# Output projections of two attention-like blocks as three products of split operands in place of one fp32 product

## The reference

```python
for l in range(DEPTH):                      # 2
    z = rmsnorm(x, g_mix[l]) @ w_in[l]      # 1024 -> 3080
    c_b, c_c, c_v, q, k, v, f_logit = jnp.split(z, SPLITS, axis=-1)
    y_conv = rmsnorm per 64 channels of short_gated_conv(c_b, c_c, c_v, conv_w[l])   # 512 channels
    y_fox = rmsnorm per head of forgetting_attention(q, k, v, log_f)                 # 8 heads x 64
    x = x + jnp.concatenate([y_conv, y_fox], axis=-1) @ w_out[l]                     # 1024 -> 1024
    hx, m = rmsnorm(x, g_xa[l]), rmsnorm(mem, g_mem[l])
    x = x + mem_cross_attention(hx, m, ...) @ w_xo[l]                                # 4 heads x 128 -> 1024
    hf = rmsnorm(x, g_ffn[l])
    x = x + (swiglu(hf, ...) if l == 0 else moe_swiglu(hf, ...))                     # 2816 wide; 8 experts, top 2
```

## Time and profile before

| | |
|---|---|
| median of 3 runs | 1675.71 us (1674.78 to 1680.75) |
| profiled execution, span | 1677.9 us |
| PE, DVE, ACT busy | 93%, 60%, 50% |
| front of layer 0, layer 1 (to the first channel mixer product) | about 0 to 305 us, 510 to 823 us |
| mean granted PE clock | 0.928 |

### The profile page before, as it was taken

One profiled execution on the slowest core, in us unless ns is written; L12 is line 12 of the kernel. 1 busy time (PEld: TensorE's weight loads), 2 busy tenths in 40 slices (PEclk: granted clock), 3 DMA queues, 4 the chain that ended last, 5 costly groups with the idle time before them and its releaser, 6 DMA issues.

```text
span 1677.9 us, 19256 instructions
## 1 busy us (share of the span) xinstructions
PE 1553.3 (93%) x7547; PEld 1257.9 (75%) x7547; DVE 1013.2 (60%) x820; ACT 844.6 (50%) x730; POOL 58.0 (3%) x59
## 2 busy tenths in 40 slices
PE   6999987899997999977799999999999999999998
PEld 5987654778877977655778777787777877778776
DVE  3334233444344334333578788787787877878777
ACT  4423222443433313222476766766677666676674
POOL 3020000000001020000000000000000000000000
PEclk8987789899997978788699999999999999999999
DMA  8321041445542412031298988989889798897987
GB/s 279 126 76 51 25 169 35 175 152 201 197 151 75 139 64 76 29 141 69 103 357 296 340 334 305 361 291 341 343 301 354 297 345 334 309 352 293 340 345 287
DMA packets 86444, 371.48 MB, mean 221 GB/s; under 512 B 7444, under 2 KB 36224, under 8 KB 69504
## 3 DMA queue, kind: packets, MB, share of 16 engines
q1 hardware_dynamic: 86400, 370.84, 60.1%
HBM read 369.78 MB, written 1.05 MB: 221 GB/s over the span
## 4 chain that ended last, share of the span: by engine, by line
PE 80%; DVE 7%; ACT 6%; issue 5%; SPq 1%; DVEq 0%; POOL 0%; DMA 0%; POOLq 0%; ACTq 0%
PE bank L1232 41%; PE bank L1228 18%; PE bank L1229 18%; ACT wh L617 3%; DVE wl L861 2%; ACT ffn L813 1%; PE bank L1240 1%; DVE ffn L1176 1%; DVE xres L1197 1%; ACT aT L646 1%; DVE xn L844 1%; DVE scratch L978 0%; ACT L614 0%; ACT xn L607 0%; PE bank L1394 0%
## 5 line engine op out<-in xcount | busy, mean ns | idle before, releaser
L861 DVE TENSOR_TENSOR wl<-ring,wh 128x2816 fp32r<-128x2816 f32 (+2 forms) x245 | 751.4, 3076 | 294.7 <-ACT wh L617 279.4
L617 ACT ACTIVATE wh<-ring 128x2816 fp32r<-128x2816 f32 (+2 forms) x245 | 623.0, 2549 | 446.3 <-PE bank L1229 355.0
L1228 PE MATMUL bank<-wh,xh 128*128 128x512 f32 (+1 forms) x960 | 364.7, 380 | 17.9 <-issue 7.3
L1229 PE MATMUL bank<-wh,xl 128*128 128x512 f32 (+1 forms) x960 | 355.9, 377 | 0.0
L1228 PEld LDWEIGHTS bank<-wh,xh 128*128 128x128 f32 x960 | 181.9, 189 | 71.5 <-DVE xres L1197 11.2
L1232 PE MATMUL bank<-wl,xh 128*128 128x512 f32 (+1 forms) x960 | 227.9, 375 | 0.0
L1229 PEld LDWEIGHTS bank<-wh,xl 128*128 128x128 f32 x960 | 182.0, 190 | 32.1
L1232 PEld LDWEIGHTS bank<-wl,xh 128*128 128x128 f32 x960 | 171.1, 189 | 27.6
L1228 PE MATMUL bank<-wh,ah 128*128 128x512 f32 x440 | 173.0, 393 | 0.8 <-DVE al L878 0.8
L1229 PE MATMUL bank<-wh,al 128*128 128x512 f32 x440 | 171.3, 389 | 0.0
L1232 PE MATMUL bank<-aT,wh 128*128 128x256 f32 x448 | 116.8, 296 | 2.1 <-DVE aT_low L879 2.1
(11 more groups left out here) (212 smaller groups left out, 1338.7 us busy)
## 6 DMA issues: line engine op xcount, KB each, us to landing
ring<-in_we_gate SPq DMA_DIRECT2D x68, 1408.0 KB, 7.2
ring<-in_we_up SPq DMA_DIRECT2D x64, 1408.0 KB, 7.9
ring<-in_we_down SPq DMA_DIRECT2D x56, 1536.0 KB, 7.9
ring<-in_w_in SPq DMA_DIRECT2D x16, 1536.0 KB, 7.7
ring<-in_w_gate SPq DMA_DIRECT2D x8, 1408.0 KB, 6.1
ring<-in_w_up SPq DMA_DIRECT2D x8, 1408.0 KB, 5.9
ring<-in_w_down SPq DMA_DIRECT2D x6, 1536.0 KB, 6.4
ring<-in_w_xkv SPq DMA_DIRECT2D x8, 1024.0 KB, 5.2
```

What stands on the lines that cost most here:

```text
L617: nc.scalar.activation(wh[:, j, 0:n], ring[:, slot, 0:n], ACT.Copy).then_inc(high_ready, 1)
L861: nc.vector.tensor_tensor(wl[:, j, 0:n], ring[:, slot, 0:n], wh[:, j, 0:n].bitcast(F32), ALU.subtract).then_inc(low_ready, 1)
L1228: nc.tensor.matmul(dst, x_high, w_high, start=first, stop=False)
L1229: return nc.tensor.matmul(dst, x_low, w_high, start=False, stop=False)
```

## The change

All fills, those of `wo` and `xo` too, are now split, so that the two buffers of `wh` and `wl` are also used for them, and their ring slots are free when the low half is made. The operand `yT` is gone. For the convolution's half DVE scales in place in `zc`, ACT copies to `aT`, and DVE subtracts into `aT_low`. For the attention's half ACT scales from the bank into `aT`, DVE subtracts into `aT_low`. For the memory attention's output ACT copies from the bank to `aT`, DVE subtracts into `aT_low`. `token_projection` makes, for each slot of two k tiles, 16 products with the high half of the weights (activation high and low) and then 8 with the low half.

```diff
     used_count, slots_used_total = {}, 0
-    split_names = [n for n in fill_names if n[1] not in ("wo", "xo")]
+    split_names = fill_names
     split_at = {n: i for i, n in enumerate(split_names)}
...
         mem_gained = xn[:].rearrange("p t (k s) -> p (t k) s", s=S)
-        yT = xn[:].rearrange("p t (k s) -> p (t k) s", s=S)
         xsc = part(5120, XH, 2, S)
...
         acthigh_ready = sem("acthigh_ready")
+        yconv_ready = sem("yconv_ready")
+        yhigh_ready = sem("yhigh_ready")
+        ylow_ready = sem("ylow_ready")
         stored = sem("stored")
...
                     nc.scalar.activation(pT[:, h, :], bank(l, f"pt{h}")[:, 0:3 * P], ACT.Copy).then_inc(take(l, f"pt{h}"), 1)
+                high_of(l, "wo", 0, 1)
+                for i in range(2):
+                    act.wait_ge(*full(l, f"mv{i}"))
+                act.wait_ge(yconv_ready, l + 1)
+                for i in range(2):
+                    nc.scalar.activation(aT[:, 2 * i:2 * i + 2, :], zc[:, 2 * i:2 * i + 2, :], ACT.Copy).then_inc(yhigh_ready, 1)
                 for i in range(2):
...
+                high_of(l, "wo", 2, 3)
+                for i in range(2):
+                    act.wait_ge(*full(l, f"oT{i}"))
+                    for k in range(2):
+                        c = 4 + 2 * i + k
+                        ins = nc.scalar.activation(aT[:, c, :], bank(l, f"oT{i}")[:, k * S:k * S + S], ACT.Copy,
+                                                   scale=col(l, "fox", 2 * i + k))
+                    ins.then_inc(yhigh_ready, 1)
                 high_of(l, "xq", 0, 1)
...
                 square(l, "xq", sq[:, 0:4, :], zqk[:, 0:4, :])
+                high_of(l, "xo", 0, 1)
                 guess_rows(l, "xq", "ssxq", mxq[:])
...
                     act.wait_ge(*full(l, f"xo{i}"))
-                    nc.scalar.activation(zqk[:, 4 + 2 * i:6 + 2 * i, :].rearrange("p a s -> p (a s)"),
-                                         bank(l, f"xo{i}")[:], ACT.Copy).then_inc(take(l, f"xo{i}"), 1)
+                    nc.scalar.activation(aT[:, 2 * i:2 * i + 2, :].rearrange("p a s -> p (a s)"),
+                                         bank(l, f"xo{i}")[:], ACT.Copy).then_inc(yhigh_ready, 1)
...
                     for j in (2 * i, 2 * i + 1):
-                        ins = nc.vector.scalar_tensor_tensor(yT[:, j, :], zc[:, j, :], col(l, "cv", j),
+                        ins = nc.vector.scalar_tensor_tensor(zc[:, j, :], zc[:, j, :], col(l, "cv", j),
                                                              bank(l, f"bc{i}")[:, (j % 2) * S:(j % 2) * S + S], ALU.mult, ALU.mult)
                     ins.then_inc(take(l, f"bc{i}"), 1)
+                for i in range(2):
+                    dve.wait_ge(*taken(l, f"bc{i}"))
+                nc.vector.engine_nop().then_inc(yconv_ready, 1)
                 for i in range(2):
...
                 probs_out(4, 6)
+                low_of(l, "wo", 0, 1)
+                for i in range(2):
+                    dve.wait_ge(yhigh_ready, 6 * l + i + 1)
+                    act_low(aT_low[:, 2 * i:2 * i + 2, :], zc[:, 2 * i:2 * i + 2, :], aT[:, 2 * i:2 * i + 2, :]).then_inc(ylow_ready, 1)
                 for q in range(2):
...
                 for i in range(2):
-                    dve.wait_ge(*full(l, f"oT{i}"))
-                    nc.vector.tensor_tensor(yT[:, 4 + 2 * i:6 + 2 * i, :], bank(l, f"oT{i}")[:].rearrange("p (k s) -> p k s", k=2),
-                                            bcast_last(col(l, "fox", 2 * i, 2), S), ALU.mult).then_inc(take(l, f"oT{i}"), 1)
+                    dve.wait_ge(yhigh_ready, 6 * l + i + 3)
+                    for k in range(2):
+                        c = 4 + 2 * i + k
+                        ins = act_low(aT_low[:, c, :], bank(l, f"oT{i}")[:, k * S:k * S + S], aT[:, c, :], col(l, "fox", 2 * i + k))
+                    ins.then_inc(take(l, f"oT{i}"), 1)
+                low_of(l, "wo", 2, 3)
                 low_of(l, "xq", 0, 1)
...
                                           ).then_inc(take(l, f"xq{i}"), 1)
+                low_of(l, "xo", 0, 1)
                 refine_rows(l, "xq", "ssxq", mxq[:])
...
                                           ).then_inc(take(l, f"xpt{h}"), 1)
+                for i in range(2):
+                    dve.wait_ge(yhigh_ready, 6 * l + i + 5)
+                    act_low(aT_low[:, 2 * i:2 * i + 2, :].rearrange("p a s -> p (a s)"), bank(l, f"xo{i}")[:],
+                            aT[:, 2 * i:2 * i + 2, :].rearrange("p a s -> p (a s)")).then_inc(take(l, f"xo{i}"), 1)
                 add_residual(l, "xw")
...
-                def token_projection(names, fill, rows, ks, src, waits):
-                    for k in ks:
-                        w = weights(l, fill, k // 2)
-                        for n in waits.get(k, ()):
-                            pe.wait_ge(*taken(l, n))
-                        for i in range(4):
-                            t, half = i // 2, i % 2
+                def token_projection(names, fill, rows, ss, waits):
+                    for s in ss:
+                        n = split_at[l, fill, s]
+                        pe.wait_ge(low_ready, n + 1)
+                        if s in waits:
+                            pe.wait_ge(*waits[s])
+                        products = [(k, i, slice(i // 2 * P, i // 2 * P + P), (k % 2) * D + (i % 2) * BANK)
+                                    for k in (2 * s, 2 * s + 1) for i in range(4)]
+                        for k, i, ts, c in products:
                             ps = open_bank(l, f"{names}{i}") if k == 0 else bank(l, f"{names}{i}")
-                            ins = mm(ps[:], src[:, k, t * P:t * P + P], w[:, k % 2, half * BANK:half * BANK + BANK],
-                                     k == 0, k == rows - 1)
+                            ins = both(ps[:], aT[:, k, ts], aT_low[:, k, ts], wh[:, n % 2, c:c + BANK], k == 0)
+                        ins.then_inc(highs_used, 1)
+                        for k, i, ts, c in products:
+                            ins = mm(bank(l, f"{names}{i}")[:], aT[:, k, ts], wl[:, n % 2, c:c + BANK], False, k == rows - 1)
                             if k == rows - 1:
                                 ins.then_inc(done(l, f"{names}{i}"), 1)
-                        if k < rows - 1 and k % 2 == 1:
+                        if 2 * s + 2 < rows:
                             ins.then_inc(slots_used, 1)
...
-                token_projection("wo", "wo", KT, range(4), yT, {0: ("bc0", "bc1")})
+                token_projection("wo", "wo", KT, range(2), {s: (ylow_ready, 2 * l + s + 1) for s in range(2)})
                 pe.wait_ge(onorm_ready, l + 1)
...
                     ins.then_inc(done(l, f"oT{i}"), 1)
-                token_projection("wo", "wo", KT, range(4, KT), yT, {4: ("oT0",), 6: ("oT1",)})
+                token_projection("wo", "wo", KT, range(2, 4), {s: taken(l, f"oT{s - 2}") for s in (2, 3)})
...
                     ins.then_inc(done(l, f"xo{i}"), 1)
-                token_projection("xw", "xo", XH, range(XH), zqk[:, 4:8, :], {0: ("xo0",), 2: ("xo1",)})
+                token_projection("xw", "xo", XH, range(2), {s: taken(l, f"xo{s}") for s in range(2)})
...
```

## The result

The changed kernel took **1687.84 us** (median of 6 runs, 1683.66 to 1688.80), the kernel before, on the same chip, 1675.93 (6 runs, 1672.68 to 1680.93). The ratio is 1.0061, with a 95% interval of 1.0046 to 1.0077: slower by about 10.3 us (the medians themselves differ by 11.9), where 10.7 had been forecast. The profiled execution has a span of 1686.9 us, 9.0 more than that of before.

The account below looks back on a forecast made before the run. PE time looked like the currency (93% busy, 80% of the chain), but in-order queues expose preparation: +2.6 +3.15 -1.55 = +4.2 a layer, +8.4, plus 2.3 for the clock: +10.7, 1686.4 us; range 1679 to 1692.

Parts of the forecast that it names:

- PE's work: Both output projections: split records 0.2265 us apart, 5.44 us a slot for 6.86, saving 17.0 us of PE over twelve slots.
- First half: Mixer projection's first products to the transposes: 12.5 us in place of 15.5, transposes 3.0 us early.
- Gap: PE's wait between the attention-output transposes and wo 2: 4.6 us, ended by DVE's low half of wo 2.
- Products of wo 2 and additions: Mixer's second half: PE needs 11.0 us, then xq 1's low half delays four additions to 234.45, before 231.87.
- Query: Memory query: xo's high halves between square and logarithm take 3.82 us, only 0.68 covered, +3.1 us a layer.
- Output: Memory output projection: PE 11.0 us for 13.90, additions sticking out 1.3 us more, -1.55 us a layer.
- I take one of two: +2.3: New gap before wo 2: the clock falls in one of two layers, slowing wo 2's products by 2.3 us.
- fourth case: Rival: clock falls in both layers' gaps before wo 2, and later also; +13 to +16 us, chance 0.24.
- the longer gap leaves a cold start that may last 1 or 2 us longer: Gap before the memory query, 8.8 us against 4.58: low clock behind it may last 1 or 2 us longer.
- Behind the fronts nothing changes order, and the delay passes through: After each layer's front: order stays the same and the fronts' delay, +8.4 us for both, passes through.
- the added splits are hidden: Mixer's first half: ACT and DVE preparation lies under the attention's PE products, costing nothing; without that cover, 8 us.

Follow-up runs that it names:

- C: Changed kernel with DVE's low half of wo 2 moved ahead of the subtractions from the attention's transposed output; 1679.80 us, ratio 1.0020.
- warm: Changed kernel with five thrown-away PE products between the attention-output transposes and wo 2, nothing moved; 1682.94 us, ratio 1.0037.
- xo only: Changed kernel with only the memory attention's projection split, the mixer's as before the change; 1676.98 us, ratio 1.0000.
- A: Changed kernel with ACT's two high halves of xo moved ahead of the memory query's square; 1681.10 us, ratio 1.0029.
- A+B+C: Changed kernel with all three moves, A, B and C, together; 1669.03 us, ratio 0.9953.
- B: Changed kernel with DVE's low half of xq 1 moved behind the four additions of the mixer's residual; 1685.61 us, ratio 1.0058.
- A+C: Changed kernel with moves A and C, xq 1's low half left ahead of the additions; 1672.98 us, ratio 0.9974.
- after again: The changed kernel, unchanged, in a second profiled execution; 1686.45 us.
- wo only: Changed kernel with only the mixer's projection split, the memory attention's as before the change; 1689.06 us, ratio 1.0071.
- banks kernels: A+B+C with output projections' last slot bank by bank, xq 1's low half later, squares relocated: 1669.73 us; also with the last edit: 1661.88 us.
- the last edit: ACT's high half of xq 1 moved behind the norm's two squares, against the bank-by-bank kernel of 1669.73 us; 1661.88 us, ratio 0.9915.

## Why the prediction was right, and where it was not

**The terms that held.** *PE's work*: spacing 0.2275 for 0.2265; 15.4 us less busy for 17.0. *First half*: 2.85 us shorter in layer 0, 3.0 forecast. *Gap*: 1.48 becomes 5.42, idle 4.38 for 4.6, ended by `wl` as said. *Products of wo 2 and additions*: 16.2 us with the clock up (C, warm), against 14.79. Together -2.85 + 3.94 + 1.4 = +2.5 us a layer; forecast 2.6. *Query*: 2.98 by the order (xo only, 28.85 for 25.86, its clock as before's); forecast 3.1. *Output*: 18.25 becomes 16.53 in the kernels whose clock is up there, -1.72, of which 1.6 is from the projection's first product on (14.72 to 13.10); forecast -1.55. By these the order costs +3.75 a layer, +7.5 in all, for +8.4. A, C and A+B+C show that each place is a cause, not a companion; for B the total says little and the stages (A+C) much.

**The clock's fall: mis-sized.** The step "I take one of two: +2.3" failed. Ten gaps of 5.4 us start to start (4.38 idle) were left empty, in five profiles (after, after again, A, B, wo only). In nine the clock fell inside the gap, 0.4 to 1.3 us before its end, and in the tenth 0.45 us behind it; in the ten of 2.5 us (C, A+B+C, A+C, both banks kernels) and the two filled ones it never did. It cost 2.8 and 2.6 us in the two layers of the profiled execution, +5.4 for +2.3. Over the ten it cost 2.6 to 2.8 us where it fell more than 0.8 us before the gap's end, and 1.3 to 1.6 where it fell later. The tenth is layer 1 of after again, where wo 2 begins at 722.08:

```profile
717.90:722.00 4.10, 0.00 (x0) 0.00 (x0) 3.84 (x6) 0.96 (x3) 0.00 (x0) 1.00 0.00 0
722.10:722.50 0.40, 0.40 (x2) 0.36 (x3) 0.40 (x1) 0.00 (x0) 0.00 (x0) 1.00 0.00 0
722.60:725.90 3.30, 3.30 (x9) 2.52 (x9) 1.62 (x1) 0.00 (x0) 0.00 (x0) 0.50 0.75 264
```

The prediction took the edge of 4.58 us as a coin toss, since it saw the clock up for most of it. The place did move, once to just past the gap's end, but the fall came each time. The rule named beside it, in the Trainium skill ("TensorE: Matmul & The Clock Gate", Why this matters for your kernels), says that idle stretches between bursts bring the lower clock. The traces agree, ten of ten, and the fourth case should have had the larger chance.

**The query: the clock went the other way.** The fourth case also had a step of its own, "the longer gap leaves a cold start that may last 1 or 2 us longer". It went the other way. The first products behind the earlier trace rows ran at the low clock to 244.5. In after the gap is 8.77 us long, the transposes end it at 243.08 with the clock low, and it is back up by 247.7:

```profile
247.70:249.00 1.30, 1.18 (x8) 1.02 (x8) 1.30 (x4) 0.00 (x0) 0.00 (x0) 1.00 0.00 0
```

so the query's products, which begin at 247.82, run fast, and "to log" is +2.0 for +3.1 in both layers. In layer 0 it was lost again: from the broadcast of the query's norms to the transposes of its probabilities 10.74 us became 12.27 (12.35 and 12.18 in layer 1). Over both fronts the two come to nothing.

**The router stretch: not in the prediction.** "Behind the fronts nothing changes order, and the delay passes through" was true of the order and not of the time. In layer 1, between the last norm and the first expert product, the same instructions take 31.70 us before and 27.66 after, and so again in the second execution of each. The records are the same, and so is PE's idle time (12.28 and 12.29 us); only its busy time differs, by 4.05. The whole stretch in before and in after:

```profile
791.32:823.02 31.70, 19.42 (x94) 18.93 (x95) 13.28 (x44) 10.38 (x18) 0.94 (x2) 0.60 0.26 91
```

```profile
805.57:833.23 27.66, 15.37 (x94) 14.88 (x95) 13.29 (x44) 10.38 (x18) 0.94 (x2) 0.69 0.15 53
```

And a part of it in each, 7.5 and 7.9 us into it:

```profile
798.80:806.50 7.70, 7.70 (x35) 7.56 (x35) 0.00 (x0) 0.83 (x2) 0.00 (x0) 0.50 0.00 0
```

```profile
813.50:817.50 4.00, 4.00 (x33) 3.93 (x32) 0.00 (x0) 0.38 (x2) 0.00 (x0) 0.91 0.02 4
```

35 records in 7.7 us and 33 in 4.0. The clock makes the -4.05.

**Sum.** The profiled spans differ by +9.0. The two fronts, mixer projection to the norm behind the memory output, give +13.0 (7.8 and 5.2), which is near the order's 7.5 and 5.4 of clock in the gaps; forecast were 8.4 and 2.3. The rest gives -4: router stretch -4.05, experts -1.2, between the layers -0.8, and the code ahead of layer 0's mixer projection +2.1 (PE makes the same products there and is idle for 22.9 us where it was for 22.7, so the added splits are hidden as forecast; the projection begins anywhere from 197.75 to 202.24 in these profiles). So 1687.8 for 1686.4 is in part luck: fronts under-priced by 2.3, and 4 us gained where nothing had been forecast. The same shifts bear on why xo only stands at 1.0000, though they are read from one execution, which was slower than its median: by the order it should be 2 x (2.98 - 1.72) = +2.5, but its router stretch is 2.7 shorter, and so is layer 1's front by 0.6 where the order alone asks for 1.3 more. And wo only, whose router stretch stayed at 31.57, stands above after (+11.9 for +10.3, intervals overlapping).

**What stays open.** Why the clock is up in the router stretch in some kernels (27.6), for part of it in others (29.0) and down for longest in before, wo only and the banks kernels (31.3 to 31.7). In the two kernels that were profiled twice it goes with the kernel and not with the execution, but no run here separated the length of the gaps ahead of it from its start time. The gain of A+B+C over the sum of the three (18.1 for 12.8), and that of the last edit over its stage (6.2 for 3.4), may be of the same kind or chance: neither is clear of the noise, and they were not split up.

## What to carry to other kernels

Before replacing one engine's work by less work that two others prepare, write out for each in-order queue what stands between the new operand and the engine that waits; here three pieces of 2 to 4 us, each one step out of place, outweighed 15 us of PE time saved, and moving them brought 18 us back. Put the preparation of the next weights into a queue's own waits, never ahead of the last dependent step, and look after each move for the next instruction that has become the late one. Count an idle gap of PE by its length plus the low-clock products behind it, and judge an order edit by its stage, and by the next one, when totals differ by less than the clock's own shifts.

## What the runs showed of the hardware

- The low clock's place largely belongs to the kernel. Stages that hold the same instructions take 31.70 and 31.71 us in two executions of before, 27.66 and 27.63 in two of after; and edits in the fronts ahead move them by 2.6 to 4 us. A few do vary from one execution to the next (15.51 and 13.79).
- Five products of 384 columns whose result is thrown away (ten records, 3.39 us) in a gap kept the clock at 1.00 through the 48 records behind it, worth 2.6 to 2.8 us a layer.
- A tiny step on POOL (128x2) took 0.95 us where DVE's subtraction on 128x2048 ran beside it: in all four layers of B and A+B+C, against 0.22 in all 24 of the other profiles at the same place. It ended just behind that subtraction, and PE's transposes came 0.74 us later. What holds it up is not shown.
- On ACT the logarithm begins 0.02 us after the table load ends (265.90 + 1.28, 267.20) with nothing else to wait for, and the load itself begins 0.02 us after the copy before it ends (262.19 + 3.69). The Trainium skill ("ScalarE: Activation LUTs", What ACT_TABLE_LOAD costs) adds a drain of 1.38 us to each switch; in the earlier trace rows a wait for PE might have hidden it, here nothing could, and it is not there.
